# 128-wide transposes of a hybrid decoder step read their tile and the identity as float32r

## What is computed

```python
h   = rms_norm(x, norm_g)                       # (1024 + 8) x 1024
p   = h @ w_in                                  # q, k, v, gates, pooling input, z
o_a = fox_attention(...)                        # 4 heads, causal, cumulative forget bias
o_b = nsa_attention(...)                        # compressed + selected + window branches, 4 heads
o_c = pool_mix(...)                             # trailing means over 2, 4, 8, 16 positions
o_m = mem_attention(q_mem, mem_prompt @ w_mem)  # 4 heads over 256 memory tokens
y   = rms_norm(x + (silu(z) * concat(o_a, o_b, o_c, o_m)) @ w_out, final_g)
```

## Time and profile before

| what | value |
|---|---|
| median of 3 runs | 813.32 us (812.92 to 816.46) |
| the profiled execution, its own time | 815.61 us |
| span of the profile | 813.9 us |
| TensorE matmul busy | 757.0 us (93%), 5664 instructions |
| VectorE / ScalarE / GpSimd busy | 378.3 / 279.8 / 170.5 us |
| mean granted TensorE clock | 0.978 |
| DMA | 81.52 MB |

### The profile page before, as it was taken

One profiled execution on the slowest core, in us unless ns is written; L12 is line 12 of the kernel. 1 busy time (PEld: TensorE's weight loads), 2 busy tenths in 40 slices (PEclk: granted clock), 3 DMA queues, 4 the chain that ended last, 5 costly groups with the idle time before them and its releaser, 6 DMA issues.

```text
span 813.9 us, 15202 instructions
## 1 busy us (share of the span) xinstructions
PE 757.0 (93%) x5664; PEld 638.7 (78%) x5664; DVE 378.3 (46%) x828; ACT 279.8 (34%) x638; POOL 170.5 (21%) x165
## 2 busy tenths in 40 slices
PE   2999987998998999999989999799999999999996
PEld 2899865996767999999856776599978788777773
DVE  3742364325772301313368888638731126524334
ACT  5522363223671303211156666502122226312111
POOL 4146640242220421320220011225222220000000
PEclk9999999999998999998989999999999999999998
DMA  7523300353304455220500000003425678365521
GB/s 270 147 73 97 73 9 14 82 152 115 140 1 127 150 146 169 59 79 27 169 2 3 2 1 2 2 18 80 117 72 163 181 206 248 122 198 176 179 81 55
DMA packets 101880, 81.52 MB, mean 100 GB/s; under 512 B 10013, under 2 KB 95276, under 8 KB 101736
## 3 DMA queue, kind: packets, MB, share of 16 engines
q1 hardware_dynamic: 100352, 79.74, 32.2%
q10 hardware_dynamic: 1456, 0.82, 0.4%
HBM read 70.91 MB, written 13.87 MB: 104 GB/s over the span
## 4 chain that ended last, share of the span: by engine, by line
PE 79%; ACT 6%; issue 4%; DVE 4%; DMA 3%; SPq 2%; POOL 2%; POOLq 0%; DVEq 0%; ACTq 0%
PE PS L554 16%; PE PS L556 15%; PE PS L555 15%; PE PS L707 6%; PE PS L670 5%; PE PS L770 4%; PE PS L686 3%; PE PS L991 2%; ACT AUG L1137 2%; PE PS L711 1%; DMA OB<-in_x_prompt 1%; PE PS L904 1%; POOL WL L1989 1%; PE PS L548 1%; ACT PP L1244 1%
## 5 line engine op out<-in xcount | busy, mean ns | idle before, releaser
L554 PE MATMUL PS<-HH,WH 128*128 128x344 f32 (+1 forms) x752 | 259.2, 345 | 6.5 <-issue 1.8
L556 PE MATMUL PS<-HH,WL 128*128 128x344 f32 (+1 forms) x752 | 253.0, 336 | 0.0
L555 PE MATMUL PS<-HL,WH 128*128 128x344 f32 (+1 forms) x752 | 252.9, 336 | 0.0
L554 PEld LDWEIGHTS PS<-HH,WH 128*128 128x128 f32 x752 | 144.4, 192 | 19.8 <-issue 7.0
L555 PEld LDWEIGHTS PS<-HL,WH 128*128 128x128 f32 x752 | 144.2, 192 | 5.9 <-issue 0.5
L556 PEld LDWEIGHTS PS<-HH,WL 128*128 128x128 f32 x752 | 144.2, 192 | 5.7
L1987 POOL TENSOR_TENSOR WH<-WR,onesc 128x1024 fp32r<-128x1024 f32 x31 | 60.8, 1960 | 345.0 <-PE PS L556 216.4
L1244 ACT ACTIVATE PP<-PP,stat 128x640 f32<-128x640 f32 (+7 forms) x96 | 70.8, 739 | 29.2 <-DVE stat L1511 29.2
L1989 POOL TENSOR_TENSOR WL<-WR,WH 128x1024 fp32r<-128x1024 f32 x31 | 76.6, 2470 | 2.4
L670 PE MATMUL PS<-AUG 64*128 64x512 f32 (+3 forms) x288 | 57.9, 507 | 4.8 <-DVE stat L1511 2.8
L686 PE MATMUL PS<-identr,PR 128*128 128x128 f32 x472 | 56.0, 255 | 4.1 <-ACT AUG L1137 2.9
(11 more groups left out here) (347 smaller groups left out, 947.3 us busy)
## 6 DMA issues: line engine op xcount, KB each, us to landing
WR<-in_w_in SPq DMA_DIRECT2D x26, 512.0 KB, 5.2
PP<-in_nsa_w SPq DMA_DIRECT2D x16, 512.0 KB, 4.4
OB<-in_x_prompt SPq DMA_DIRECT2D x8, 512.0 KB, 6.6
out<-NAT SPq DMA_DIRECT2D x2, 2048.0 KB, 7.7
PP<-in_cache_fox_kv SPq DMA_DIRECT2D x32, 128.0 KB, 2.2
WR<-in_x_prompt SPq DMA_DIRECT2D x8, 512.0 KB, 4.2
out<-PP SPq DMA_DIRECT2D x8, 512.0 KB, 2.9
out<-in_state_nsa_win SPq DMA_DIRECT2D x1, 4088.0 KB
```

Of the source, the lines that this page charges most:

```text
L554: mm(out, lhs[0], rhs[0], start=(k == 0), stop=False)
L555: mm(out, lhs[0], rhs[1], start=False, stop=False)
L556: return mm(out, lhs[1], rhs[0], start=False, stop=(k == KC - 1))
```

## The change

A helper `twin` makes a second name of type float32r for the bytes that the next tensor gets (it opens a tensor, keeps its handle and closes it again, so the next one lies at the same address). `AUG`, `XT`, `KW` and `OB` get such names, `PP`'s is written the same way. The transposes of lines 548, 637, 639, 643, 646, 711, 857 and 966 read them with `identr` in place of `ident`, and name their PSUM output as float32r. Nothing else is changed: the transposes of small tiles (754, 816, 875, 879, 952, 970, 971), all waits and all copies stay.

```diff
--- before.py
+++ after.py
@@ -177,6 +177,11 @@
         def sb(name, shape, dt=F32):
             return ctx.enter_context(nc.sbuf_tensor(name, shape, dt))
 
+        def twin(name, shape):
+
+            with nc.sbuf_tensor(name, shape, F32R) as same_bytes:
+                return same_bytes
+
         def sem(name):
             return ctx.enter_context(nc.semaphore(name))
 
@@ -189,16 +194,19 @@
         WR = sb("WR", [P, 2, KC, P])
         WH = sb("WH", [P, 2, KC, P], F32R)
         WL = sb("WL", [P, 2, KC, P], F32R)
+        AUGR = twin("AUGR", [P, 8, TT])
         AUG = sb("AUG", [P, 8, TT])
+        XTR = twin("XTR", [P, TT])
         XT = sb("XT", [P, TT])
         NAT = sb("NAT", [P, NQ * 512])
         VW = sb("VW", [P, NQ * P])
+        KWR = twin("KWR", [P, 4 * P])
         KW = sb("KW", [P, 4 * P])
         with nc.sbuf_tensor("MR", [P, 2, KC, NMEM], F32R) as mem_rows:
             mth, mtl = mem_rows[:, 0, :, :], mem_rows[:, 1, :, :]
-        with nc.sbuf_tensor("PR", [P, 4 * 1024], F32R) as turned_rows:
-            PPR = turned_rows[:, :]
+        PPR = twin("PR", [P, 4 * 1024])
         PP = sb("PP", [P, 4 * 1024])
+        OBR = twin("OBR", [P, 4096 + NJ * (R_ALL + 1)])
         OB = sb("OB", [P, 4096 + NJ * (R_ALL + 1)])
         ident = sb("ident", [P, P])
         identr = sb("identr", [P, P], F32R)
@@ -263,6 +271,12 @@
             if UNITS[u][0] == "fox":
                 return KW[:, u % 2 * P:(u % 2 + 1) * P], KW[:, 256:256 + P]
             return XT[:, u % 2 * P:(u % 2 + 1) * P], XT[:, 512:512 + P]
+
+        def sums_twin(u):
+
+            if UNITS[u][0] == "mem":
+                return KWR[:, u % 2 * 256:(u % 2 + 1) * 256]
+            return (KWR if UNITS[u][0] == "fox" else XTR)[:, u % 2 * P:(u % 2 + 1) * P]
 
         def item_dst(rows_x, rows_mem, i, half):
 
@@ -537,16 +551,16 @@
                 rows = NB if i == 8 else P
                 if i < 9:
                     pe.wait_ge(s_xn, i + 1)
-                    src = xn[0:rows, i % 2, :]
+                    src = OBR[0:rows, 4096 + i % 2 * 1024:4096 + (i % 2 + 1) * 1024]
                 else:
                     pe.wait_ge(s_x[i % 4], 16 * (i // 4 + 1))
-                    src = xr[:, i % 4, :]
+                    src = OBR[:, i % 4 * 1024:(i % 4 + 1) * 1024]
                 for half in range(2):
                     if i:
                         pe.wait_ge(s_lo, 2 * i - 1 + half)
                     for k in range(4):
-                        last = tr(bk(6 + half)[:, k * P:k * P + rows],
-                                  src[:, (4 * half + k) * P:(4 * half + k + 1) * P], ident[0:rows, 0:rows])
+                        last = tr(bk(6 + half)[:, k * P:k * P + rows].bitcast(F32R),
+                                  src[:, (4 * half + k) * P:(4 * half + k + 1) * P], identr[0:rows, 0:rows])
                     last.then_inc(s_itT, 1)
 
             def passes(out, lhs, rhs, k):
@@ -634,16 +648,18 @@
                     out = spare_job(side, spare[side]) if spare else job_a() if side == 0 else job_d()
                     for n, t in enumerate(tiles):
                         if what == "memk":
-                            last = tr(out[:, n * P:(n + 1) * P], AUG[:, 6 + TILES[m][1], t * P:(t + 1) * P], ident[:, :])
+                            last = tr(out[:, n * P:(n + 1) * P].bitcast(F32R), AUGR[:, 6 + TILES[m][1], t * P:(t + 1) * P],
+                                      identr[:, :])
                         elif what == "foxk":
-                            last = tr(out[:, n * P:(n + 1) * P], AUG[:, 4 + TILES[m][1], t * P:(t + 1) * P], ident[:, :])
+                            last = tr(out[:, n * P:(n + 1) * P].bitcast(F32R), AUGR[:, 4 + TILES[m][1], t * P:(t + 1) * P],
+                                      identr[:, :])
                         elif what in ("ks", "kw"):
                             slot = {"ks": 4, "kw": 6}[what]
                             for a in range(2):
-                                last = tr(out[:, n * P + a * DH:n * P + a * DH + DH],
-                                          AUG[0:DH, slot + a, t * P:(t + 1) * P], ident[0:DH, 0:DH])
+                                last = tr(out[:, n * P + a * DH:n * P + a * DH + DH].bitcast(F32R),
+                                          AUGR[0:DH, slot + a, t * P:(t + 1) * P], identr[0:DH, 0:DH])
                         else:
-                            last = tr(out[:, n * P:(n + 1) * P], XT[:, t * P:(t + 1) * P], ident[:, :])
+                            last = tr(out[:, n * P:(n + 1) * P].bitcast(F32R), XTR[:, t * P:(t + 1) * P], identr[:, :])
                     last.then_inc(s_TA if side == 0 else s_TD, 1)
 
             def scores(u):
@@ -708,7 +724,7 @@
                            stop=(b == (1 if what == "mem" else nk - 1)))
                 pe.wait_ge(s_rb, u + 1)
                 for a in range(wide):
-                    last = tr(bk(7)[:, (2 + a) * P:(3 + a) * P], sums_at(u)[0][:, a * P:(a + 1) * P], ident[:, :])
+                    last = tr(bk(7)[:, (2 + a) * P:(3 + a) * P].bitcast(F32R), sums_twin(u)[:, a * P:(a + 1) * P], identr[:, :])
                 last.then_inc(s_pv, 1)
 
             def attend(u0, u1):
@@ -854,7 +870,7 @@
                 taken(22)
                 out = job_a()
                 for j in range(2):
-                    last = tr(out[0:15, j * P:(j + 1) * P], PP[:, j * 1056 + T:j * 1056 + T + 15], ident[:, :])
+                    last = tr(out[0:15, j * P:(j + 1) * P].bitcast(F32R), PPR[:, j * 1056 + T:j * 1056 + T + 15], identr[:, :])
                 last.then_inc(s_TA, 1)
 
             def pool_map(j):
@@ -963,7 +979,7 @@
                 pe.wait_ge(s_px, 1)
                 out = job_a()
                 for pg in range(NPG):
-                    last = tr(out[:, pg * P:(pg + 1) * P], X[:, pg * P:(pg + 1) * P], ident[:, :])
+                    last = tr(out[:, pg * P:(pg + 1) * P].bitcast(F32R), OBR[:, OT0 + pg * P:OT0 + (pg + 1) * P], identr[:, :])
                 last.then_inc(s_TA, 1)
                 mark["X"] = nA[0]
                 out = job_d()
```

## The result

Over 22 runs of each, interleaved, the kernel after took 810.65 us (808.80 to 813.98) where the kernel before took 813.83 (808.52 to 816.46). The ratio is 0.9973, with an interval of 0.9961 to 0.9985: 2.2 us faster, between 1.2 and 3.2. The forecast was 5.5 us faster, 807.8, with a range up to 811.8. The direction was right; the size is less than half, and counted by the 0.5% of the prediction it is no change.

A forecast was written before the change was run, and what follows sets the result against it. TensorE was taken to bound the kernel (busy 757.0 of 813.9 us, 79% of the chain). Terms 1.65 + 2.01 + 0 + 1.68 + 0.15 = 5.5 us, from 813.3 to 807.8 us; range 804.5 to 811.8.

The forecast's parts named there:

- 30 ns for each transpose: Price of one full 128x128 transpose at full clock: 109 ns between starts in float32 against 79 in float32r.
- Items: Line 548, transposes of the input items (80 full, 8 tiny): claimed to save 1.65 us in all.
- items 4 to 10: Line 548: items 4 and 5 half counted, 0.24 us; items 6, 7, 9 and 10 fully, 0.96 us.
- item 8: Line 548, the input item with 8 rows: too few columns to matter, taken as 0, bounded by 0.1 us either way.
- Item 3: Line 548, directly ahead of part 0 of the projections: 0.71 us, or 0.39 if the clock rises at the same moment.
- Lines 637, 639 and 646: 72 full transposes (foxv, kc, vc, vw, vs, foxk, memk, memv): claimed to save 2.01 us.
- Line 643: 24 transposes with 64 columns: taken as 0, with ends of -0.2 to +0.5 us.
- Line 711: 64 transposes of attention units' finished sums: 1.68 us, of it 1.44 in 48 wide units and 0.24 in the memory phase.
- Lines 857 and 966: 2 and 4 transposes at 30 ns each: 0.18 us, put at 0.15.
- the load that sets the pitch: Rival: weight load sets the pitch, or the same two passes are issued; gain 0.4 us, 812.9 us, chance 0.05.
- Absorption: Rival: TensorE arrives earlier and waits longer, in attention above all; gain 2 to 4 us, 810.5 us, chance 0.15.
- The signs that I had named: If right: TensorE busy time falls about 6 us, idle unchanged, line means drop 25 to 30 ns; if absorbed, idle grows.

## Why the prediction was wrong, step by step

The forecast held that TensorE bounds the kernel, that the gain would be TensorE's, and that no other engine would absorb it in attention; all of this stood. What failed is the term that was in every step: **30 ns for each transpose.**

It was read from two rows with different followers. The float32 group had float32 transposes behind it (0.87 us), the float32r group a projection (0.63). With a projection behind both it is this, float32 and then float32r:

```profile
278.98 1.04 PE L646 MATMUL PS<-ident,XT 128*128 128x128 f32 x8
279.77 0.40 PE L554 MATMUL PS<-HH,WH 128*128 128x344 f32 x1
280.02 0.32 PE L555 MATMUL PS<-HL,WH 128*128 128x344 f32 x1
```

```profile
278.60 0.80 PE L662 MATMUL PS<-identr,XTR 128*128 128x128 f32 x8
279.24 0.39 PE L568 MATMUL PS<-HH,WH 128*128 128x344 f32 x1
279.46 0.32 PE L569 MATMUL PS<-HL,WH 128*128 128x344 f32 x1
```

0.79 us against 0.64, and to the second matmul behind 1.04 against 0.86: 0.15 to 0.18 us for eight, so 19 to 22 ns each. I had like-for-like rows and took the handiest. The profile before has an item group with a projection behind it, 0.79 us again, and in the view of the earlier trace rows itself the next float32 group, line 816's, has its projection 0.80 us behind (155.60 to 156.40).

```profile
34.28 1.03 PE L548 MATMUL PS<-ident,OB 128*128 128x128 f32 x8
35.07 0.41 PE L554 MATMUL PS<-HH,WH 128*128 128x344 f32 x1
```

- *Items, 1.65 forecast:* 0.76 came, from items 4 to 10 (1.20 forecast), with 0.16 to 0.19 for eight of items 6, 7, 9 and 10 where I had 0.24, 0.19 for items 4 and 5 together (0.24), and a loss of 0.15 for item 8, which I had put at 0 and bounded by 0.1. Item 3's 0.39 hung on the condition that the clock rises at the same moment; it was there in the two profiles where the rise did, and is lost in chance in the others.
- *Lines 637, 639 and 646, 2.01 forecast:* about 1.5. Groups beside projections gave 0.16 in place of 0.24, the one in front of other float32 transposes 0.23, foxk twice 0.29 in place of 0.36; vc gave 0.07 only, because its second half waits for VectorE's copy (0.28 us, 0.16 before), and vw 0.13. vs, at the lower clock, went from 1.90 to 1.18 us and gave part of it back in the projections behind, as argued: from 376 to 386 us the lead grew by 0.44 (0.39 forecast). The price at the lower clock was right, a pitch of 213 ns in float32 and 127 in float32r.
- *Line 643, 0 forecast:* -0.25. I had bounded the loss by the wide pitch and then took 0, with the reason that both types load the same columns. That was the wrong reason: the float32r pitch is 84 ns here too, and the lower bound, -0.2, was the answer.
- *Line 711, 1.68 forecast:* 0.14, all in the memory phase (0.24 forecast there), and 0 for the 48 others (1.44 forecast). This is the step that made the forecast wrong. A price taken in a row of eight was put on a transpose that stands alone in front of ten float32r ones. These, by the reading above, need only part of their 86 ns for the pass, and a float32 transpose's longer pass goes into that slack; the distances to the fourth start show that the difference goes, and with float32 followers that it stays. The lone one's long record (334 ns, now 280) I had even counted as an upside. It shows latency, not cost.
- *Lines 857 and 966, 0.15 forecast:* 0.25.

Sum: 0.76 + 1.5 - 0.25 + 0.14 + 0.25 = 2.4 us, and up to 0.4 more where item 3 counts. The 1.9 at equal clock (1.4 to 2.4) and the 2.2 of the ratio (1.2 to 3.2) are near it.

Of the rivals, the load that sets the pitch was the nearest, if the floor is the load's, which no run shows: with 86 ns and not 107. Of its other half, that two passes are issued either way, no trace shows anything: both kernels have one matmul in the records for each transpose, 5664 matmuls in all. Absorption happened only by chance at tile 5. The signs that I had named did speak: busy time fell by 7.7 us, more than the 6 announced, while the time fell by far less. The records overlap, so a fall of busy time and of mean durations is no gain. TensorE's idle time, my sign of absorption, grew by 4.4 us: 2.1 of it in the first 23 us, where I had called the items hidden, 1.2 at tile 5, and 0.9 from 418 to 527 us, where the halved clock is missing; in the units from 193 to 252 us it did not grow, and there line 711 gave nothing all the same.

## What to carry to other kernels

Price a change of type by the distance between starts in a like group with a like follower, never by a record's length, and not by a row average when the instruction stands alone: a slow one among fast ones hides in whatever slack the fast ones have. float32r pays for transposes of 128 columns in rows, some 20 ns each; it costs at 64 and at 8 columns, some 20 ns each; it does nothing for single ones in front of float32r rows. When one execution differs from the next by more than the effect, line up the same instruction's start in two traces, and compare times at equal clock.

## What the runs showed of the hardware that was not expected

The float32r transpose with 64 identity columns is slower than the float32 one, 84 against 62 ns of pitch, and with 8 columns it is 83 against 62. And 448 more transposes in float32 went with a mean granted clock of 0.989 to 0.996, in float32r with 0.980 to 0.988, so part of a shorter pitch may be given back to the clock.
